# The causal mask of FoX attention: added in PSUM by VectorE in place of an identity product on TensorE

## Chip, core and metric

The kernel runs on one core of a Trainium2 chip. Times are device microseconds of one execution; a kernel's time is the median of its runs.

## What is computed

One block of a streaming encoder for 1024 tokens of width 1024: RMS norm, one input projection, attention heads and state-space (S5) heads side by side, one output projection, a mixture of 32 experts (the best four for each token), a gated per-layer embedding and a last norm. The change lies in the attention. Eight heads of 64 dimensions compute, for each block of 128 query rows,

```
logits = jnp.einsum('bqhd,bkhd->bhqk', q_i, k) * scale
logits = logits + c_i[..., :, None] - c_t[..., None, :]
logits = jnp.where(key_pos[None, :] <= q_pos[:, None], logits, -jnp.inf)
w = jax.nn.softmax(logits, axis=-1)
return jnp.einsum('bhqk,bkhd->bqhd', w.astype(v.dtype), v)
```

Here c is the cumulative sum of the log forget gates. Only the diagonal block of 128x128 (queries and keys of the same block) needs the mask within it; blocks beyond it aren't computed.

## The kernel before

The program is written by hand for each engine: five instruction streams, ordered by semaphores (`wait_ge`, `then_inc`). The attention stage handles 32 tiles. A tile is a pair of heads p and a query block i with i+1 key blocks; for each p the order of i is 0, 7, 1, 6, 2, 5, 3, 4 (`TILES`). Its scores come in units of up to 512 keys, one unit for i<4 and two for i≥4; a unit has two PSUM banks, one for each head of the pair, and two units' banks alternate.

A tile s passes through the engines like this:

- TensorE, `scores(s)`: q times k of both heads (L1717), and for the unit with the diagonal the mask (L1721). The unit's `s_mm` is raised by its last matmul. q carries a factor of −0.125, so the masked elements get +1e30 (`FAR`) and a minimum is the largest logit.
- VectorE, `row_low(s)` (L1198): for each unit and head one instruction reads the scores from PSUM, adds the gate sums (`cumb`), writes the result `sc` to SBUF and reduces its minimum into `low`. The profile calls it CUSTOM_DVE_ANT_0, with a small DVE_READ_ACCUMULATOR2_ANT behind it. It raises `low_ready`.
- ScalarE, `exp(s)` (L790): exp over the whole rows, one instruction for each head, with the sum `den`.
- VectorE, `recip(s)` (L1205): reciprocal of `den`; GpSimd (L626) multiplies the rows by it.
- TensorE, `turn_probs(s, part)` (L1735): 128x128 transposes into PSUM banks 4 and 5. ScalarE (L802) copies bank 4 to `probT`, VectorE's `turned_second` (L1216) copies bank 5. The next group of transposes into a bank waits for its copy.
- TensorE, `values(s)` (L1751): probT times v; VectorE's `heads_out` (L1224) copies the result to `attnT`.

The engines run ahead by three tiles. In turn s VectorE's queue holds recip(s+2), row_low(s+3), turned_second(s), heads_out(s−1), in this order; TensorE's holds scores(s+3), turn_probs(s, 0), values(s−1), turn_probs(s, 1); ScalarE's holds its copies of s and exp(s+3). GpSimd works on the GELU of the state-space heads in between. `link` raises `dve_chain` with an instruction and makes VectorE wait for it ahead of the next one.

The loop on VectorE:

```
recip(s + 2)
row_low(s + AHEAD)
turned_second(s)
heads_out(s - 1)
```

Of the kernel before, what the change touches and what calls it, by code (L numbers as in the profile page):

```python
# [23 lines left out]
ALU = mybir.AluOpType  # L24
ACT = mybir.ActivationFunctionType
F32 = mybir.dt.float32
BF16 = mybir.dt.bfloat16
# [5 lines left out]
P = 128  # L33
# [3 lines left out]
HEADS, DH = 8, 64  # L37
# [91 lines left out]
def build(nc, x_cm, x_tm, pT, small, consts, b_f, d_skipT, b_router, gains, w_in, w_glu, w_out,  # L129
          w_router, w_router_q, w_gu, w_dn, b_exp, b_gu, b_dn, w_ple_gate, w_ple_proj, out, hs, ys, cum):  # L130
    with ExitStack() as ctx:
        sem = {}

        def S(name):
            if name not in sem:
                sem[name] = ctx.enter_context(nc.semaphore(name))
            return sem[name]
# [12 lines left out]
        def at(name, shape, dt, offset):  # L150
            return nc.alloc_sbuf_tensor_at(name, shape, dt, offset=offset)

        def sb(name, shape, dt=F32):

            size = int(np.prod(shape[1:])) * (2 if dt == BF16 else 4)
            t = at(name, shape, dt, cursor[0])
            cursor[0] += (size + 31) // 32 * 32
            return t

        ps = ctx.enter_context(nc.psum_tensor("ps", [P, 8, 512], F32))  # L160
# [4 lines left out]
        ident = cst[:, O_ID:O_ID + P]  # L165
# [4 lines left out]
        tid = cst[:, O_TID:O_TID + 8]  # L170
        quad = cst[:, O_QD:O_QD + 1]
        ones = sb("ones", [P, P])
        ident_b = sb("ident_b", [P, P], BF16)
        mask_qk = sb("mask_qk", [P, P], BF16)
        bf = sb("bf", [8, 1])
        dsk = sb("dsk", [SC, NG])
# [43 lines left out]
        kA = at("kA", [P, HEADS // 2, T], F32, R_K)  # L220
# [130 lines left out]
        def scores_of(s):  # L351

            return sc01[:, s % 2] if s % 4 < 2 else sc23[:, s % 2]
# [620 lines left out]
        def _(dve):  # L974
            v = nc.vector
            chain = [0]

            def link(ins):

                chain[0] += 1  # L980
                ins.then_inc(S("dve_chain"), 1)
                dve.wait_ge(S("dve_chain"), chain[0])
# [150 lines left out]
            for n in range(2):  # L1133
                ins = v.tensor_scalar(rbc[:, 512 * n:512 * n + 512], ps[:, n, :], 1.0 / D, EPS, ALU.mult, ALU.add)
# [2 lines left out]
            v.reciprocal(rtok[:, :], rtok[:, :]).then_inc(S("rtok_ready"), 1)  # L1137
            dve.wait_ge(S("par_ld"), 16)
            dve.wait_ge(S("small_ld"), 80)
            v.tensor_copy(ident_b[:, :], ident)  # L1140
            dve.wait_ge(S("par_ld"), 16)
            dve.wait_ge(S("small_ld"), 80)
            link(v.tensor_copy(mask_qk[:, :], mask_f[:, :]))
            angles()
            coefficients()
# [3 lines left out]
            for i, un in enumerate(PROJ):  # L1149
# [20 lines left out]
                if un[0] in "kq":  # L1170
                    dst = kA if un[0] == "k" else qA
                    m, n = un[1:]
# [11 lines left out]
            def row_low(s):  # L1184


                p, i = TILES[s]
                if s >= 4:
                    dve.wait_ge(S("tr_mm"), 2 * UNITS[s - 3])
                for c in range(1 + (i >= 4)):  # L1190
                    un = UNITS[s] + c
                    w = min(512, (i + 1) * P - 512 * c)
                    dve.wait_ge(S("s_mm"), un + 1)
                    for a_ in range(2):
                        lo = low[:, s % 4, a_:a_ + 1]
                        if c:
                            dve.wait_ge(S("low_ready"), 2 * un - 1 + a_)
                        v.tensor_tensor_reduce(scores_of(s)[:, a_, 512 * c:512 * c + w], ps[:, 2 * (un % 2) + a_, 0:w],  # L1198
                                               cumb[:, p % 2, a_, 512 * c:512 * c + w], 1.0, lo if c else 3e38,
                                               ALU.add, ALU.min, lo).then_inc(S("low_ready"), 1)  # L1200
# [30 lines left out]
            for s in range(AHEAD):  # L1231
                row_low(s)
# [3 lines left out]
            for s in range(NT):  # L1236
                if s + 2 < NT:
                    recip(s + 2)
                if s and s + AHEAD < NT:
                    if (s + AHEAD) % 8 == 0:  # L1240
                        p = (s + AHEAD) // 8
# [24 lines left out]
            for n in range(8):  # L1266
                co, hf = n // 2, n % 2
# [126 lines left out]
            for c, w in enumerate(WIDTHS):  # L1394
                less = [i for i in range(NW) if WIDTHS[i] < w]
                if less:
                    i = max(less, key=lambda i: WIDTHS[i])
                    ins = v.tensor_tensor(cmask[:, c, 0:32], cown[:, i, 0:32], cown[:, c, 0:32], ALU.subtract)
                else:
                    ins = v.tensor_scalar(cmask[:, c, 0:32], cown[:, c, 0:32], -1.0, 1.0, ALU.mult, ALU.add)  # L1400
# [39 lines left out]
            for q in range(4):  # L1440
                c = slice(8 * q, 8 * q + 8)
# [150 lines left out]
        def _(pe):  # L1592
            m = nc.tensor
# [64 lines left out]
            for n in range(2):  # L1658
                ins = m.matmul(ps[:, n, :], ones[:, :], sqa[:, 512 * n:512 * n + 512], start=True, stop=True)
            ins.then_inc(S("sq_mm"), 1)  # L1660
            pe.wait_ge(S("h_ready"), KT)
            for t in range(4):
                for k in range(KT // 2, KT):
                    ins = u_step(t, k)
                ins.then_inc(S("pj_mm"), 1)
                if t == 1:
# [3 lines left out]
                    for c in range(16):  # L1670
                        toks = rbc[:, c:T:CH] if c < 8 else rbc[:, (c - 8) * P:(c - 7) * P]
                        ins = m.transpose(ps[:, (0, 1, 6, 7)[c // 4], (c % 4) * P:(c % 4) * P + P], toks, ident)
                    ins.then_inc(S("rtok_mm"), 1)
            for i, un in enumerate(PROJ):
# [5 lines left out]
                if un[0] == "u":  # L1680
                    for k in range(KT):
                        ins = m.matmul(ps[:, bank, :], hT[:, k, un[1]:T:CH], w_u[:, k, :], start=(k == 0), stop=(k == KT - 1))  # L1682
                elif un[0] == "v":
                    if un[1] == 0:
                        pe.wait_ge(S("wv_ld"), 32)
                    for k in range(KT):
                        ins = m.matmul(ps[:, bank, :], hT[:, k, un[1] * P:un[1] * P + P], w_v[:, k, :], start=(k == 0), stop=(k == KT - 1))  # L1687
                elif un[0] == "f":
                    for k in range(KT):

                        j = 32 * (k % 4)
                        ins = m.matmul(ps[j:j + 8, bank, :], wf[:, k, :], hT[:, k, 512 * un[1]:512 * un[1] + 512], start=(k < 4), stop=(k >= 4))
                else:
# [3 lines left out]
                    for k in range(KT):  # L1697
                        ins = m.matmul(ps[:, bank, :], w_[:, k, un[1] * P:un[1] * P + P], hT[:, k, 512 * un[2]:512 * un[2] + 512],  # L1698
                                       start=(k == 0), stop=(k == KT - 1))
# [5 lines left out]
            def scores(s):  # L1705


                p, i = TILES[s]
                for c in range(1 + (i >= 4)):
                    un = UNITS[s] + c  # L1710
                    if un >= 2:
                        pe.wait_ge(S("low_ready"), 2 * un - 2)
                    w = min(512, (i + 1) * P - 512 * c)
                    diag = (i * P) // 512 == c
                    for a_ in range(2):
                        hf = DH * a_
                        ins = m.matmul(ps[:, 2 * (un % 2) + a_, 0:w], qA[hf:hf + DH, p, i * P:i * P + P],  # L1717
                                       kA[hf:hf + DH, p, 512 * c:512 * c + w], start=True, stop=not diag)
                    if diag:
                        for a_ in range(2):  # L1720
                            ins = m.matmul(ps[:, 2 * (un % 2) + a_, w - P:w], ident_b[:, :], mask_qk[:, :], start=False, stop=True)  # L1721
                    ins.then_inc(S("s_mm"), 1)

            def turn_probs(s, part):
# [53 lines left out]
            for n in range(8):  # L1778
                co, hf = n // 2, n % 2
                if n >= 2:  # L1780
                    pe.wait_ge(S("gl_sig"), n - 1)
                for k in range(4):
                    ins = m.matmul(ps[:, 4 + n % 2, :], wglu[:, k, co * P:co * P + P], gT[:, k, hf * 512:hf * 512 + 512],  # L1783
                                   start=(k == 0), stop=(k == 3))
# [141 lines left out]
            for q in range(4):  # L1926
                pe.wait_ge(S("tok_ready"), 2 * q + 2)
                for c in range(8 * q, 8 * q + 8):
# [3 lines left out]
                    ins = m.matmul(ps[:, 1, at_:at_ + P], ohr[:, c, :], ohc[:, :, :].rearrange("p c n -> p (c n)")[:, lo:lo + P],  # L1932
                                   start=(c == 0), stop=(c == 31), skip_group_check=True)
# [4 lines left out]
            for r in range(4):  # L1938
                ins = m.matmul(ps[:, 6, nh * r:nh * r + nh], selq[:, r, :, :].rearrange("p a j -> p (a j)"), rowid[:, :], start=True, stop=True,
                               skip_group_check=True)  # L1940
# [75 lines left out]
            for i in range(16):  # L2016
# [4 lines left out]
                for k in range(2):  # L2021
                    ins = m.matmul(ps[:, 4 + i % 4, :], ppT[:, k, i // 2, :], wpp[:, k, 512 * (i % 2):512 * (i % 2) + 512], start=(k == 0), stop=(k == 1))
# [105 lines left out]
```

## Time and profile before

| | before |
|---|---|
| median of three runs | 2180.05 us (2179.83 to 2181.12) |
| profiled execution | 2180.62 us, of which span 2179.1 us |
| TensorE (PE) busy | 2120.1 us, 97% |
| VectorE (DVE) busy | 1005.8 us, 46% |
| ScalarE (ACT) busy | 374.4 us, 17% |
| GpSimd (POOL) busy | 599.2 us, 27% |
| mean granted TensorE clock | 0.993 |

The span goes from the first to the last instruction of the profiled execution. PE is TensorE's matmul side. The experts take the greater part of the span; the attention stage lies between about 275 and 406 us. In the rows a time in front is the start in us from the span's start; "[0.45 <-ACT sc L790]" behind a row says that the engine was idle for 0.45 us before it and what ended the wait. Durations of matmuls overlap with the next ones.

### The profile page before, as it was taken

The numbers are of one execution on the slowest core, as the hardware profiler recorded it, in microseconds if no ns is written. First come the engines' busy times: TensorE is split into PE (matmuls) and PEld (weight loads), VectorE is DVE, ScalarE is ACT, GpSimd is POOL, SyncE is SP. The second block draws the span as 40 slices with busy tenths as digits, with TensorE's granted clock in tenths as the row PEclk, the third lists the DMA queues.
The fourth block names the chain that finished last, engine by engine and source line by source line (L and its number), as shares of the span: only waits on it lengthen the run. The fifth ranks groups of instructions, "written<-read, shape, count | busy, mean of one in ns | idle before, by whom it ended". The sixth has DMA issues, their size and how long they took to land.

```text
span 2179.1 us, 53600 instructions
## 1 busy us (share of the span) xinstructions
PE 2120.1 (97%) x21898; PEld 1704.4 (78%) x21898; DVE 1005.8 (46%) x2155; ACT 374.4 (17%) x769; POOL 599.2 (27%) x905
## 2 busy tenths in 40 slices
PE   8999999999799999999999999999999999999998
PEld 5555566544478999999787889798999999999443
DVE  4665467534854544454343332623233333443474
ACT  3120056510411101000110100100000000000344
POOL 0465678300133122222212211213111231212420
PEclk9999999999999999999999999999999999999999
DMA  5100011512299999999999974989667888885740
GB/s 209 44 21 12 6 59 32 197 52 74 97 360 417 416 418 398 367 374 348 351 340 334 332 283 177 384 334 351 233 230 245 291 310 311 307 319 189 268 166 39
DMA packets 101816, 528.18 MB, mean 242 GB/s; under 512 B 22326, under 2 KB 26214, under 8 KB 49614
## 3 DMA queue, kind: packets, MB, share of 16 engines
q1 hardware_dynamic: 76894, 465.58, 56.9%
q0 software_dynamic: 24816, 61.12, 8.1%
q8 instruction: 75, 1.23, 0.2%
q14 instruction: 31, 0.25, 0.0%
HBM read 496.06 MB, written 27.30 MB: 240 GB/s over the span
## 4 chain that ended last, share of the span: by engine, by line
PE 90%; DVE 3%; issue 3%; ACT 2%; DMA 1%; POOL 1%; SPq 0%; POOLq 0%; DVEq 0%; ACTq 0%
PE ps L1963 23%; PE ps L1960 20%; PE ps L1978 14%; PE ps L1698 5%; PE ps L2001 4%; PE ps L2038 3%; PE ps L1991 3%; PE ps L1803 3%; PE ps L1687 3%; PE ps L1810 2%; PE ps L1717 1%; PE ps L1751 1%; PE ps L1783 1%; PE ps L1682 1%; PE ps L1735 1%
## 5 line engine op out<-in xcount | busy, mean ns | idle before, releaser
L1963 PE MATMUL ps<-xT,wg 128*64 128x112 f32 (+5 forms) x10752 | 504.5, 257 | 11.7 <-issue 8.3
L1963 PEld LDWEIGHTS ps<-xT,wg 128*64 128x64 f32 x10752 | 499.8, 138 | 20.3 <-issue 20.3
L1960 PE MATMUL ps<-xT,wg 128*128 128x144 f32 (+5 forms) x3072 | 434.8, 304 | 0.0
L1960 PEld LDWEIGHTS ps<-xT,wg 128*128 128x128 f32 x3072 | 430.0, 190 | 4.5 <-issue 1.3
L1510 DVE TENSOR_SCALAR gb<-ps,bcur 128x256 f32<-128x256 f32 x264 | 127.7, 484 | 559.9 <-PE ps L1963 287.5
L1978 PE MATMUL ps<-actT,wd 128*64 128x112 f32 (+6 forms) x3584 | 317.8, 278 | 0.0
L1978 PEld LDWEIGHTS ps<-actT,wd 128*64 128x64 f32 (+1 forms) x3584 | 313.8, 160 | 1.6
L920 ACT ACTIVATE sg<-gb 128x256 f32<-128x256 f32 x264 | 110.0, 417 | 1131.4 <-DVE gb L1510 1131.4
L639 POOL DMA_INDIRECT xg<-normalised_rows,rowc x184 | 178.5, 970 | 76.8 <-issue 49.1
L669 POOL COPY rowc<-rowq 128x8 uint32 (+1 forms) x34 | 6.4, 190 | 593.6 <-DVE xT L1475 591.0
L1500 DVE TENSOR_TENSOR tb<-gb,sg 128x256 f32<-128x256 f32 x264 | 112.2, 425 | 42.4 <-ACT sg L920 42.4
L1523 DVE STREAM_TRANSPOSE yb<-ps 128x1024 f32<-128x1024 f32 x20 | 25.0, 1250 | 230.4 <-PE ps L1978 230.4
L1511 DVE TENSOR_SCALAR ub<-ps,bcur 128x256 f32<-128x256 f32 x264 | 125.4, 475 | 0.0
L1503 DVE SCALAR_TENSOR_TENSOR actT<-ub,tb 128x256 f32<-128x256 f32 x264 | 112.1, 425 | 9.1
L2038 PE MATMUL ps<-wpg,xnT 128*128 128x512 f32 x256 | 112.4, 595 | 2.4 <-ACT xnT L933 2.4
L685 POOL DMA_DIRECT2D bin__188<-in_b_exp x33 | 18.9, 573 | 311.1 <-issue 311.1
L2001 PE MATMUL ps<-wd,actT 128*128 128x512 f32 x224 | 98.0, 595 | 0.0
L2038 PEld LDWEIGHTS ps<-wpg,xnT 128*128 128x128 f32 x256 | 47.5, 190 | 61.6 <-issue 54.5
L2001 PEld LDWEIGHTS ps<-wd,actT 128*128 128x128 f32 x224 | 42.0, 190 | 51.4 <-issue 51.4
L1475 DVE STREAM_TRANSPOSE xT<-xg 128x1024 f32<-128x1024 f32 x66 | 78.0, 1219 | 0.0
L696 POOL DMA_DIRECT2D expert_rows<-yb x80 | 46.6, 584 | 91.6 <-DVE yb L1525 69.9
L1991 PE MATMUL ps<-wd,actT 128*32 128x256 f32 x1024 | 57.7, 380 | 1.8 <-issue 1.8
(417 smaller groups left out, 2140.2 us busy)
## 6 DMA issues: line engine op xcount, KB each, us to landing
wg<-in_w_gu SPq DMA_DIRECT2D x264, 1024.0 KB, 7.3
wd<-in_w_dn SPq DMA_DIRECT2D x132, 1024.0 KB, 7.6
expert_rows<-yb POOLq DMA_DIRECT2D x60, 128.0 KB, 5.6
expert_rows<-yb POOLq DMA_DIRECT2D x28, 160.0 KB, 5.4
hT<-in_x_cm SPq DMA_DIRECT2D x8, 512.0 KB, 8.5
cumb<-gate_sums SPq DMA_DIRECT2D x4, 1024.0 KB, 4.8
x<-in_x_tm SPq DMA_DIRECT2D x1, 4096.0 KB, 13.7
wout<-in_w_out SPq DMA_DIRECT2D x1, 4096.0 KB, 21.0
```

The costliest lines, as they stand in the source:

```text
L639: g.indirect_dma_start(xg[:, half, DQ * r:DQ * r + DQ], None, hs[:, :], bass.IndirectOffsetOnAxis(ap=rows[:, r, half:half + 1], axis=0)).t ...
L920: a.activation(sg[:, f % 2, :], gb[:, f % 2, :], ACT.Sigmoid, scale=1.702).then_inc(S("sig_ready"), 1)
L1500: v.tensor_tensor(tb[:, f % 2, :], gb[:, f % 2, :], sg[:, f % 2, :], ALU.mult).then_inc(S("tb_ready"), 1)
L1503: v.scalar_tensor_tensor(actT[:, f, :], ub[:, f % 2, :], -6.0, tb[:, f % 2, :], ALU.max, ALU.mult).then_inc(S("act_ready"), 1)
L1510: v.tensor_scalar(gb[:, f % 2, :], ps[:, f % 2, 0:W], bcur[:, f:f + 1], 7.0, ALU.add, ALU.min).then_inc(S("g_ready"), 1)
L1511: v.tensor_scalar(ub[:, f % 2, :], ps[:, f % 2, W:2 * W], bcur[:, 8 + f:9 + f], 8.0, ALU.add, ALU.min).then_inc(S("gu_evac"), 1)
L1960: ins = m.matmul(ps[:, f % 2, g_ * W:g_ * W + w], wg[:, f, k, g_, :], xT[:, k, 0:w], start=(k == 0), stop=(k == KT - 1))
L1963: ins = m.matmul(ps[c:c + 64, f % 2, g_ * W:g_ * W + w], wg[:, f, k, g_, c:c + 64], xT[:, k, 0:w], start=(k == 0), stop=(k == KT - 1))
L1978: ins = m.matmul(ps[c:c + cols, 2 + o_ // 2, W * (o_ % 2):W * (o_ % 2) + w], wd[:, f, P * o_ + c:P * o_ + c + cols], actT[:, f, 0:w], star ...
L1991: ins = m.matmul(ps[GR * j:GR * j + GR, 2 + r // 2, 256 * (r % 2):256 * (r % 2) + 256], actT[:, f, GR * r:GR * r + GR], down_cols(f, j, 1) ...
L2001: ins = m.matmul(ps[:, 2 + c, :], actT[:, f, 0:P], down_cols(f, 2 * c, 2), start=(f == 0), stop=(f == FT - 1))
L2038: ins = m.matmul(ps[:, 2 + n, :], xnT[:, t % 2, k, :], wpg[:, k, n * 512:n * 512 + 512], start=(k == 0), stop=(k == KT - 1))
```

## The change

TensorE's two products of the identity with the mask go from `scores`; the scores' matmuls then end their group themselves. `row_low` gets one VectorE instruction ahead of the reductions of the unit with the diagonal: it adds the mask (bf16, the same for both heads) to the last 128 columns of both banks, in place in PSUM, and is linked, so the reduction waits for its end. The bf16 copy of the identity, `ident_b`, and its conversion are dropped.

```
@@ scalars, once @@
-            v.tensor_copy(ident_b[:, :], ident)
-            dve.wait_ge(S("par_ld"), 16)
-            dve.wait_ge(S("small_ld"), 80)
             link(v.tensor_copy(mask_qk[:, :], mask_f[:, :]))
@@ row_low @@
                     dve.wait_ge(S("s_mm"), un + 1)
+                    if (i * P) // 512 == c:
+                        at_diag = ps[:, 2 * (un % 2):2 * (un % 2) + 2, w - P:w]
+                        link(v.tensor_tensor(at_diag, at_diag, mask_qk[:, :].unsqueeze(1).to_broadcast([P, 2, P]), ALU.add))
                     for a_ in range(2):
@@ scores @@
-                    diag = (i * P) // 512 == c
                     for a_ in range(2):
                         hf = DH * a_
                         ins = m.matmul(ps[:, 2 * (un % 2) + a_, 0:w], qA[hf:hf + DH, p, i * P:i * P + P],
-                                       kA[hf:hf + DH, p, 512 * c:512 * c + w], start=True, stop=not diag)
-                    if diag:
-                        for a_ in range(2):
-                            ins = m.matmul(ps[:, 2 * (un % 2) + a_, w - P:w], ident_b[:, :], mask_qk[:, :], start=False, stop=True)
+                                       kA[hf:hf + DH, p, 512 * c:512 * c + w], start=True, stop=True)
                     ins.then_inc(S("s_mm"), 1)
```

VectorE's queue at the tiles i=5 and i=3, before: the first tile's four reductions (ISA is the reduction of L1198, the row behind it reads the accumulator), the copies of probT and attnT, the reciprocal, and the next tile's reductions and copy.

```order
L1198 ISA sc_96,low<-ps,cumb,low 128x256 [waits low_ready,s_mm]
L1198 ISA low 128x1
L1198 ISA sc_96,low<-ps,cumb,low 128x256 [waits low_ready]
L1198 ISA low 128x1
L1216 COPY probT<-ps 128x256 [waits tr_mm,pv_mm]
L1224 COPY attnT<-ps 128x16x8 [waits pv_mm]
L1205 RECIPROCAL rden<-den 128x2 [waits exp_done]
L1198 ISA sc_97,low<-ps,cumb 128x512 [waits s_mm,tr_mm]
L1198 ISA low 128x1
L1198 ISA sc_97,low<-ps,cumb 128x512
L1198 ISA low 128x1
L1216 COPY probT<-ps 128x384 [waits tr_mm,pv_mm]
```

The same place now, up to the second reduction of i=3 (lines behind the addition are one lower in the file, L1192 is the addition):

```order
L1192 TENSOR_TENSOR ps<-ps,mask_qk 128x2x128 [waits s_mm]
L1197 ISA sc_95,low<-ps,cumb,low 128x256 [waits low_ready,dve_chain]
L1197 ISA low 128x1
L1197 ISA sc_95,low<-ps,cumb,low 128x256 [waits low_ready]
L1197 ISA low 128x1
L1215 COPY probT<-ps 128x256 [waits tr_mm,pv_mm]
L1223 COPY attnT<-ps 128x16x8 [waits pv_mm]
L1204 RECIPROCAL rden<-den 128x2 [waits exp_done]
L1192 TENSOR_TENSOR ps<-ps,mask_qk 128x2x128 [waits s_mm,tr_mm]
L1197 ISA sc_96,low<-ps,cumb 128x512 [waits dve_chain]
L1197 ISA low 128x1
L1197 ISA sc_96,low<-ps,cumb 128x512
```

An addition has come in ahead of the second unit of i=5 and one between the reciprocal and the reductions of i=3; the waits for `s_mm` and `tr_mm` moved to it. The copy of 128x384 stands behind both.

TensorE's queue in the turn with the scores of i=3, before: scores, mask, transposes of the tile i=6, values of i=1, transposes again.

```order
L1717 MATMUL ps<-kA,qA 128x512 [waits low_ready]
L1717 MATMUL ps<-kA,qA 128x512
L1721 MATMUL ps<-mask_qk,ident_b 128x128 x2
L1735 MATMUL ps<-cst,sc_97 128x128 [waits ta_evac,pn_ready]
L1735 MATMUL ps<-cst,sc_97 128x128 x3
L1735 MATMUL ps<-cst,sc_97 128x128 [waits tb_evac,pn_ready]
L1735 MATMUL ps<-cst,sc_97 128x128 x2
L1751 MATMUL ps<-probT,vA 64x128 [waits at_evac,tb_evac,ta_evac]
L1751 MATMUL ps<-probT,vA 64x128 x3
L1735 MATMUL ps<-cst,sc_97 128x128 [waits ta_evac,pn_ready]
L1735 MATMUL ps<-cst,sc_97 128x128 x2
L1735 MATMUL ps<-cst,sc_97 128x128 [waits tb_evac,pn_ready]
```

The same turn now:

```order
L1715 MATMUL ps<-kA,qA 128x512 [waits low_ready]
L1715 MATMUL ps<-kA,qA 128x512
L1730 MATMUL ps<-cst,sc_96 128x128 [waits ta_evac,pn_ready]
L1730 MATMUL ps<-cst,sc_96 128x128 x3
L1730 MATMUL ps<-cst,sc_96 128x128 [waits tb_evac,pn_ready]
L1730 MATMUL ps<-cst,sc_96 128x128 x2
L1746 MATMUL ps<-probT,vA 64x128 [waits at_evac,tb_evac,ta_evac]
L1746 MATMUL ps<-probT,vA 64x128 x3
L1730 MATMUL ps<-cst,sc_96 128x128 [waits ta_evac,pn_ready]
L1730 MATMUL ps<-cst,sc_96 128x128 x2
L1730 MATMUL ps<-cst,sc_96 128x128 [waits tb_evac,pn_ready]
```

Only the row of the mask is gone. The last row is a transpose that waits for VectorE's copy of probT (`tb_evac`).

## Rows read from the trace of the kernel before

**Rows 1.** Windows: stage, one head pair, idle time and half-clock spell near its start.

```profile
core 0: us, PE busy (x) PEld busy (x) DVE busy (x) ACT busy (x) POOL busy (x), PEclk, DMA share, GB/s
275.00:406.00 131.00, 123.16 (x1170) 84.30 (x1169) 93.44 (x308) 79.17 (x187) 99.19 (x117) 0.99 0.19 54
324.46:354.69 30.23, 29.11 (x283) 19.88 (x281) 22.20 (x77) 20.18 (x48) 24.34 (x30) 1.00 0.11 36
286.40:288.80 2.40, 0.00 (x0) 0.00 (x0) 0.42 (x3) 2.30 (x6) 2.40 (x3) 1.00 0.05 20
289.80:293.20 3.40, 3.40 (x15) 2.37 (x16) 1.51 (x5) 1.87 (x5) 3.22 (x6) 0.51 0.00 0
```

**Rows 2.** Chain that ended last, 346 to 353 us: start, us, what.

```profile
346.64 0.69 DVE sc L1198
...
348.53 1.85 ACT sc L790 x3
...
350.84 0.23 DVE sc L1198
...
351.88 0.61 DVE probT L1216
352.50 0.14 issue
352.63 0.41 PE ps L1735 x2
```

**Rows 3.** Groups by form, 270 to 410 us: xcount, then busy us, mean ns.

```profile
L1721 PE MATMUL ps<-mask_qk,ident_b 128*128 128x128 bf16 x64 | 9.1, 224 | 0.0
...
L1198 DVE CUSTOM_DVE_ANT_0 sc<-ps,cumb 128x256 f32<-128x256 f32 x8 | 3.1, 422 | 2.9 <-PE ps L1721 2.9
```

**Rows 4.** Timeline of TensorE, 333 to 354 us: start, us, operation.

```profile
339.68 0.29 PE L1721 MATMUL ps<-mask_qk,ident_b 128*128 128x128 bf16 x2
339.80 1.05 PE L1735 MATMUL ps<-cst,sc 128*128 128x128 f32 x8
340.77 1.53 PE L1751 MATMUL ps<-probT,vA 128*64 128x128 f32 x24
```

**Rows 5.** Timeline of VectorE, 53 to 54.7 us; L1056 waits for L1055's end.

```profile
53.65 0.42 DVE L1054 TENSOR_TENSOR t<-cf,par 128x256 f32<-128x256 f32 x1
53.99 0.42 DVE L1055 TENSOR_TENSOR t<-cf,par 128x256 f32<-128x256 f32 x1
54.44 0.43 DVE L1056 TENSOR_TENSOR par<-t,t 128x256 f32<-128x256 f32 x1
```

**Rows 6.** Groups by form of VectorE, whole span.

```profile
L1511 DVE TENSOR_SCALAR ub<-ps,bcur 128x256 f32<-128x256 f32 x264 | 125.4, 475 | 0.0
...
L1500 DVE TENSOR_TENSOR tb<-gb,sg 128x256 f32<-128x256 f32 x264 | 112.2, 425 | 42.4 <-ACT sg L920 42.4
```

**Rows 7.** Timeline of VectorE behind tile i=5, 327.9 to 330 us.

```profile
327.98 0.17 DVE L1205 RECIPROCAL rden<-den 128x2 f32<-128x2 f32 x1 [0.45 <-ACT sc L790]
328.52 0.69 DVE L1198 CUSTOM_DVE_ANT_0 sc<-ps,cumb 128x512 f32<-128x512 f32 x1 [0.37 <-PE ps L1721]
...
329.74 0.55 DVE L1216 COPY probT<-ps 128x384 f32<-128x384 f32 x1
```

**Rows 8.** Timeline of TensorE: transposes behind that copy, two later groups of scores.

```profile
330.44 0.63 PE L1735 MATMUL ps<-cst,sc 128*128 128x128 f32 x4 [0.24 <-DVE probT L1216]
...
337.75 1.99 PE L1717 MATMUL ps<-kA,qA 64*128 64x512 f32 x8
...
345.36 1.77 PE L1717 MATMUL ps<-kA,qA 64*128 64x512 f32 x8
```

**Rows 9.** Timeline of VectorE behind tile i=4, 335.6 to 337 us.

```profile
335.67 0.17 DVE L1205 RECIPROCAL rden<-den 128x2 f32<-128x2 f32 x1 [0.32 <-ACT sc L790]
...
336.25 0.08 DVE L1198 DVE_READ_ACCUMULATOR2_ANT low<- 128x1 f32 x1
336.32 0.43 DVE L1216 COPY probT<-ps 128x256 f32<-128x256 f32 x1
```

**Rows 10.** Timeline of VectorE behind tile i=7, 343.4 to 344.5 us.

```profile
343.47 0.17 DVE L1205 RECIPROCAL rden<-den 128x2 f32<-128x2 f32 x1 [0.73 <-ACT sc L790]
...
344.28 0.28 DVE L1216 COPY probT<-ps 128x128 f32<-128x128 f32 x1
```

More of the change, by code:

```diff
@@ L172, in build @@
         ones = sb("ones", [P, P])
-        ident_b = sb("ident_b", [P, P], BF16)
         mask_qk = sb("mask_qk", [P, P], BF16)
```

## Prediction

> **What bounds the kernel now.** The change touches only the attention stage, so shares of the whole span say little and I began with the windows. The stage runs from 275 to 406 us: 131 us, TensorE busy for 123.16 (94%) and VectorE for 93.44 [rows 1]. It repeats. One head pair is eight tiles and takes 30.23 us (324.46 to 354.69), with TensorE busy for 29.11 us and VectorE for 22.20 [rows 1]. By these sums VectorE has 8 us to spare in each head pair and TensorE 1.1. A sum doesn't tell where idle time lies, so I went on to the chain of waits. Around the tiles i=6 and i=2 it leaves TensorE for 6 us: VectorE reduces, ScalarE exponentiates, VectorE takes the reciprocal, reduces tile i=2, copies probT, and only then does TensorE transpose [rows 2]. So the reader is to see a loop with one turn per tile: reduction, exp, reciprocal, the next tile's reduction. The copy that TensorE waits for stands in VectorE's queue behind that reduction.
>
> **What is removed.** 64 matmuls of the mask go, two in each of 32 tiles [rows 3]. Their 224 ns are mostly latency. What they take from TensorE is the distance from their start to the next group's: 339.68 to 339.80 [rows 4]. That is 0.12 us a tile, 32 × 0.12 = 3.8 us if nothing else changes. It counts only where TensorE is itself the limit; at a place where it waits for the copy of probT, an earlier arrival is only a longer wait. One conversion (ident_b, half of 128x256) at the start of the program goes as well; it can't be worth more than an operation of twice its size, 0.42 us [rows 5], and as the coefficients behind it wait for an exp of ScalarE I count it at nothing.
>
> **What is added.** 32 additions on VectorE over 128x256 elements, each with a wait of the next reduction for its end. No row shows VectorE writing PSUM, so I bound the price d per tile. Read from PSUM, the shape takes 422 ns as a reduction [rows 3]; the addition of two SBUF operands takes 425 [rows 6]. With a wait behind it the next operation starts 0.45 us later (53.99 to 54.44); without one, 0.34 (53.65 to 53.99) [rows 5]. Lower end of d: 0.34, if the wait cost nothing. Upper end: 475 ns for the slowest operation of this shape from PSUM [rows 6], plus the 0.03 between an end and a waiting start (54.41 to 54.44): 0.51. I take 0.45, because the addition is nearest to the TENSOR_TENSOR rows with a wait, and the reduction shows no surcharge for a PSUM source.
>
> The Trainium skill does put one on it ("VectorE: DVE Perf Modes", section on the TRN2 errata): 120 fixed cycles from PSUM against 58 from SBUF, at 0.96 GHz, thus an estimated 0.065 us more. This trace disagrees for reads (422 ns from PSUM, 425 from SBUF). By that rule d would be 0.52 and the sum 10.2 us, by the rows it is what follows.
>
> **Where d lands.** The addition stands ahead of the reduction whose end starts both exps. With i≥4 ScalarE starts as soon as the reduction has ended, so a whole d passes through the exps into the reciprocal; the next tile's addition comes behind that reciprocal, and then the copy of probT. The tiles thus work in pairs, and TensorE waits for the copy behind the second: 2d less the slack that the rows show. The copy's end reaches a transpose 0.14 us later (329.74 + 0.55 = 330.29 to 330.44; 351.88 + 0.61 to 352.63) [rows 7, 8, 2].
>
> - Pair (5,3), four times: the reciprocal runs at 327.98, and the reduction of i=3 could follow 0.15 later but starts at 328.52, when the mask matmul has ended [rows 7]. Slack 0.40; the transposes at 330.44 wait for the copy already [rows 8]. 2d − 0.40 = 0.50.
> - Pair (4,0), three times (the last tile, i=4, has no partner): the copy starts at 336.32, 0.07 after VectorE is free at 336.25, and ends at 336.75; with 0.14 it would allow transposes at 336.89 [rows 9]. The four that need it start about 337.26: the next group starts at 337.75 [rows 8], and four transposes take 0.49 (eight from 339.80 to 340.77 [rows 4]). Slack 0.36 + 0.07. 2d − 0.43 = 0.47.
> - Pair (7,1), three times: the copy ends at 344.56 [rows 10], allows 344.70, and the four start near 345.36 − 0.49 = 344.87 [rows 8]. 2d − 0.16 = 0.74. The reciprocal ahead of it waited 0.73 for the exps of i=7 [rows 10].
> - Pair (6,2), three times: no slack, both additions stand on the chain as it is [rows 2]. 2d = 0.90.
>
> The first pairs (7,1) and (6,2) don't count: from 286.40 to 288.80 TensorE is idle for 2.40 us while GpSimd, busy throughout, is late with its normalisation, and right after it TensorE runs at half clock (0.51 granted from 289.80 to 293.20, that is 1.2 GHz of 2.4) [rows 1]; VectorE's 0.9 us hides there. At every waiting place TensorE's own saving since the last wait disappears, so it is not subtracted. The sum is 4×0.50 + 3×0.47 + 3×0.74 + 3×0.90 = 8.3 us, in general 26d − 3.4; 0.1 for the last tile's copy makes 8.4. Nothing behind the stage hides it: by the code everything later hangs on the last tile's values. Against the profiled execution (span 2179.1, 2180.62 in all) that gives 2189.0; the median of the runs lies 0.57 below it, so I predict **2188.5 us**. The bounds of d give 5.5 and 10.0 us, 2185.6 and 2190.1.
>
> **Rivals.**
> - *VectorE's idle time takes it in.* 32 × 0.45 = 14.4 us fit in 131 − 93.4 = 37.6 us idle [rows 1], TensorE stays the limit and gains 3.8 us: 2176.2, not slower. It decides if the slack of every pair is 0.9 us or more. For it speaks TensorE's share of 94%; against it, that three pairs of a head pair show less than 0.5 and the fourth none. Chance 0.06, half of it for over 0.2% (should each mask matmul free the 0.22 us of its duration, 7 us). [...]
> - *Only the second addition counts.* If the first of a pair is taken in before the reciprocal, a place costs d less its slack. At (5,3), where the start then hangs on the scores, which come 0.12 earlier, it is 0.33, and 0.02, 0.29 and 0.45 at the others: 1.3 + 0.1 + 0.9 + 1.3 = 3.6 us, 2183.7, within 0.2%. Against it: the reciprocal waits for ScalarE in the pairs (0.45, 0.32 and 0.73 us [rows 7, 9, 10]). Chance 0.12.
> - *The addition is dearer*, with a penalty for writing PSUM and reading it at once: at d = 0.6 it is 12.2 us, 2192.3. Chance 0.06.
> - *The clock falls more often.* The half-clock spell of 3.4 us followed an idle time of 2.4 us; the new waits stay under 1 us. A spell costs at most 1.7 us; one more gives 2190.2, three 2193.6. Chance 0.07.
>
> **How the numbers follow.** My case has 0.69. A measurement of this kernel tells about 0.2% (4.4 us) from no change. Slower by over that: 0.69 + 0.06 + 0.07 = 0.82. Same: 0.12 + 0.03 = 0.15. Faster: 0.03. The range 2183.0 to 2193.0 takes in the second rival, the bounds of d, d = 0.6 and one or two more spells.
>
> **What would show it.** In the profile after: no L1721; 32 TENSOR_TENSOR on ps with 0.42 to 0.48 us, the reduction behind them 0.45 to 0.5 after their start; the eight tiles in about 32.8 us in place of 30.2 (30.2 + 0.50 + 0.47 + 0.74 + 0.90); about 8 us more idle time of TensorE before its transposes, released by VectorE's probT copy; the expert stage unchanged. A period of 30 us or less would refute the pairs; an unchanged period with a longer span would point at the clock.

## Result, and the profile after

The changed kernel takes **2189.77 us** (median of six runs, 2186.93 to 2191.90), the kernel before 2180.87 in the same comparison (six runs, 2179.83 to 2182.95). The ratio is 1.0041, 95% interval 1.0030 to 1.0051: 8.9 us slower, where 8.4 were forecast against the profiled execution. The sum came out right, but not all of its terms: in the profiled execution three half-clock spells came in, and 4.6 us came back in the experts, where I had expected nothing.

The page of the changed kernel, span and busy times:

```profile
span 2187.9 us, 53502 instructions
...
PE 2123.9 (97%) x21834; PEld 1706.5 (78%) x21834; DVE 1017.3 (46%) x2186; ACT 374.0 (17%) x769; POOL 599.4 (27%) x905
```

VectorE is busy for 11.5 us more. TensorE is too, for 3.8 us, with 64 products fewer: the first sign that its clock has to do with it. The totals don't show where the 8.8 us lie by which the span grew, so the windows come next: two periods of eight tiles, the place where TensorE waits longest in a period, and what its clock does behind it.

```profile
core 0: us, PE busy (x) PEld busy (x) DVE busy (x) ACT busy (x) POOL busy (x), PEclk, DMA share, GB/s
...
307.12:341.64 34.52, 30.91 (x276) 20.32 (x272) 24.97 (x85) 20.17 (x49) 26.79 (x32) 0.95 0.09 30
341.64:375.84 34.20, 30.23 (x264) 19.67 (x261) 25.01 (x86) 19.66 (x48) 26.26 (x32) 0.95 0.07 28
322.90:325.90 3.00, 1.08 (x10) 0.66 (x9) 2.16 (x7) 2.19 (x6) 2.26 (x3) 1.00 0.00 0
326.60:330.00 3.40, 3.40 (x14) 1.53 (x12) 2.53 (x9) 0.72 (x3) 3.22 (x5) 0.50 0.00 0
```

A period was 30.23 us at a clock of 1.00 [rows 1]. Now it is 34.20 to 34.52 at 0.95: more than the forecast 32.8. VectorE has 25.0 us of work in a period in place of 22.2, still 9 us short of it. The last row is new in kind: 3.40 us at a granted clock of 0.50, 1.2 of 2.4 GHz, and it comes in three of the four periods (326.63, 360.76 and 394.90 us).

Groups by form of the changed kernel, 270 to 420 us (the additions; the transposes):

```profile
L1730 PE MATMUL ps<-cst,sc 128*128 128x128 f32 x288 | 46.9, 293 | 16.3 <-POOL sc L625 6.0 <-ACT probT L801 5.3 <-DVE probT L1215 4.6
...
L1192 DVE TENSOR_TENSOR ps<-ps,mask_qk 128x256 f32<-128x256 f32 x32 | 13.7, 430 | 3.4 <-PE ps L1715 3.3
```

The addition takes 430 ns in place, within 5 ns of the same shape in SBUF [rows 6]. TensorE's idle time ahead of the transposes is 16.3 us; before, it was 6.6 in the same group, so 9.7 us were added.

VectorE's timeline of the changed kernel around the first such place, behind the tiles i=6 and i=2:

```profile
320.06 0.43 DVE L1192 TENSOR_TENSOR ps<-ps,mask_qk 128x256 f32<-128x256 f32 x1
320.52 0.62 DVE L1197 CUSTOM_DVE_ANT_0 sc<-ps,cumb,low 128x384 f32<-128x384 f32 x1
...
323.38 0.17 DVE L1204 RECIPROCAL rden<-den 128x2 f32<-128x2 f32 x1 [1.18 <-ACT sc L789]
323.46 0.43 DVE L1192 TENSOR_TENSOR ps<-ps,mask_qk 128x256 f32<-128x256 f32 x1
323.92 0.56 DVE L1197 CUSTOM_DVE_ANT_0 sc<-ps,cumb 128x384 f32<-128x384 f32 x1
...
324.88 0.69 DVE L1215 COPY probT<-ps 128x512 f32<-128x512 f32 x1
```

From the start of an addition to the reduction that waits for it are 0.46 us, both times. The first addition stands ahead of the exps (idle 1.18 until their end), the second between the reciprocal and the copy of probT. TensorE's timeline of the changed kernel there:

```profile
322.73 0.44 PE L1746 MATMUL ps<-probT,vA 128*64 128x128 f32 x4
324.49 0.63 PE L1730 MATMUL ps<-cst,sc 128*128 128x128 f32 x4 [1.32 <-ACT probT L801]
325.72 0.63 PE L1730 MATMUL ps<-cst,sc 128*128 128x128 f32 x4 [0.60 <-POOL sc L625]
```

and the same tiles in the kernel before, some 3 us earlier:

```profile
321.61 0.63 PE L1735 MATMUL ps<-cst,sc 128*128 128x128 f32 x4 [0.70 <-ACT probT L802]
322.41 0.63 PE L1735 MATMUL ps<-cst,sc 128*128 128x128 f32 x4 [0.18 <-DVE probT L1216]
```

The idle time grew from 0.88 to 1.92 us here: 0.62 behind ScalarE's copy, which stands behind the exps and so gets one addition (and what the mask's products no longer fill), and 0.42 behind VectorE's copy, which gets the second.

### The profile page after: what moved, and what is told of

The parts are those of the page before. It is cut to its first block, busy times and chain, and to the rows that moved or that the text cites. A ratio compares the mean times of both kernels' runs of the same rounds, so it can differ in the third digit from the quotient of the medians.

```text
span 2187.9 us, 53502 instructions
## 1 busy us (share of the span) xinstructions
PE 2123.9 (97%) x21834; PEld 1706.5 (78%) x21834; DVE 1017.3 (46%) x2186; ACT 374.0 (17%) x769; POOL 599.4 (27%) x905
## 4 chain that ended last, share of the span: by engine, by line
PE 88%; DVE 4%; issue 3%; ACT 2%; DMA 1%; POOL 1%; SPq 0%; POOLq 0%; DVEq 0%; ACTq 0%
PE ps L1958 23%; PE ps L1955 20%; PE ps L1973 14%; PE ps L1697 5%; PE ps L1996 4%; PE ps L2033 3%; PE ps L1986 3%; PE ps L1798 3%; PE ps L1686 3%; PE ps L1805 2%; PE ps L1715 1%; PE ps L1778 1%; PE ps L1681 1%; DVE x L1537 1%; PE ps L1730 1%
## 5 line engine op out<-in xcount | busy, mean ns | idle before, releaser
L1958 PEld LDWEIGHTS ps<-xT,wg 128*64 128x64 f32 x10752 | 497.2, 138 | 18.7 <-issue 18.7
L1958 PE MATMUL ps<-xT,wg 128*64 128x112 f32 (+5 forms) x10752 | 501.5, 256 | 10.4 <-issue 7.0
L1510 DVE TENSOR_SCALAR ub<-ps,bcur 128x256 f32<-128x256 f32 x264 | 125.5, 475 | 0.0
L1730 PE MATMUL ps<-cst,sc 128*128 128x128 f32 x288 | 46.9, 293 | 16.3 <-POOL sc L625 6.0
```

Of the source, the lines that this page charges most:

```text
L1510: v.tensor_scalar(ub[:, f % 2, :], ps[:, f % 2, W:2 * W], bcur[:, 8 + f:9 + f], 8.0, ALU.add, ALU.min).then_inc(S("gu_evac"), 1)
L1958: ins = m.matmul(ps[c:c + 64, f % 2, g_ * W:g_ * W + w], wg[:, f, k, g_, c:c + 64], xT[:, k, 0:w], start=(k == 0), stop=(k == KT - 1))
```

## The experiments

Two theories stood at first. The **pairs** (the prediction's): two additions on the loop through VectorE and ScalarE, less the slack of each place, and nothing else. The **clock**: the new waits make TensorE run at half clock, and this is a good part of the loss. The experts gave a third question. "End of the stage" is the end of the last tile's values, 405.97 us in the profile of before; all differences are to that profile, tile by tile, so that the stage's start, the periods and the spells can be told apart.

**Both kernels again.**

> The kernel before, profiled once more, unchanged. My reading of the first pair of traces: the attention stage ends 13.6 us later after the change (8.6 us of waits and 5.0 us for three more half-clock spells), and the experts' two memory-bound passes give back 4.6 us by chance. Chance theory: the attention stage lasts 130.7 us again (values end within 0.5 us of 405.97) while the sum of the two memory-bound expert passes (30.1 and 33.0 us in the first trace of before) moves by a us or more. Rival, the giving back is a mechanism that follows from the later start: both passes last as in the first trace, within 0.3 us.

2181.76 us (one run). Its stage ends 1.33 later: the half-clock spell at 288 us lasts 6.83 us in place of 3.41. All of the difference is there by the second tile and stays the same for the other 30. So a tile's time reproduces to 0.02 us but for the start, where the longer spell costs 1.3. The chance theory of the experts had asked for an end within 0.5 us and for passes that differ by 1 us or more; they differ by 0.54 (63.15 and 62.61 us, table below). It failed on both.

> The changed kernel, profiled once more, unchanged, timed in five rounds. Both theories: about 2189.8 us. Attention theory: last values near 419.5, period of eight tiles 34.2 to 34.5 us, three spells of half clock behind the waits at the pair (6,2). Chance theory for the experts: their two memory-bound passes differ from 27.5 and 31.0 us by a us or more in sum; rival (mechanism): they don't.

2189.43 us, ratio 1.0042 (1.0029 to 1.0056). The stage ends 12.35 later than before's, against 13.57 in the first profile of the same kernel. This one has two spells in its periods (358.70, 392.83), the first had three; up to 322 us the two differ by 0.26. The experts' two passes differ by 0.92 us from the first profile's, where the chance theory wanted 1 or more.

**Fill the wait.** Twelve transposes of the identity into a free bank, in the turns of i=7 from the second pair of heads on:

```diff
                     values(s - 1)
+                if s > 8 and TILES[s][1] == 7:
+                    pe.wait_ge(S("at_evac"), s - 1)
+                    for _ in range(12):
+                        m.transpose(ps[:, 6 + s % 2, 0:P], ident, ident)
```

> The changed kernel with 12 extra transposes of the identity on TensorE, at the three places where it waits about 1.4 us for the copy of tile i=7 (ahead of its second group of transposes); they write a PSUM bank that the next values overwrite, and leave all waits as they are. Clock theory: TensorE's idle time there is what makes the clock fall; the three spells at 326.6, 360.8 and 394.9 vanish and the time falls by up to 5 us, to about 2185. Rival (the spells come from elsewhere or cost nothing): spells stay, time 2189.8 or up to 4 us more, for the added work.

Timeline of TensorE in this kernel, the second of the three places:

```profile
357.19 1.53 PE L1768 MATMUL ps<-cst 128*128 128x128 f32 x12
358.58 0.63 PE L1730 MATMUL ps<-cst,sc 128*128 128x128 f32 x4
359.80 0.63 PE L1730 MATMUL ps<-cst,sc 128*128 128x128 f32 x4 [0.59 <-POOL sc L625]
```

The wait of 1.32 us is filled, that of 0.6 is left as it was, and no period has a spell (the ones at 361 and 395 were expected to go; the run's first, at 288 us, is the long one). The three periods and the last tiles, from 322 us on, cost 7.60 us (10.67 − 3.07); in the two profiles of the changed kernel they cost 11.31 and 10.35. So the waits alone are worth 7.6 us there, three spells 3.7 and two 2.75: 1.2 to 1.4 each. At the spell itself 1.59 is lost (2.55 in place of 0.96 from one tile to the next), and 0.35 comes back at the following wait. So the clock is a second cause, and the spells are gone where this idle time is filled. That is one profiled execution with three places, against two with five spells in six. The kernel gained nothing in all, where up to 5 us were expected (2190.36 us, ratio 1.0038, 1.0025 to 1.0052); its experts say why, below.

**The second addition moved away from the copy.** The additions of i<4 go to the front of the turn, ahead of the reciprocal, and the reduction waits for them later:

```diff
             for s in range(NT):
+                if s and s + AHEAD < NT and TILES[s + AHEAD][1] < 4:
+                    mask_early(s + AHEAD)
                 if s + 2 < NT:
```

> The changed kernel with the addition of the tiles i<4 issued ahead of the reciprocal instead of behind it; all 32 additions stay on VectorE. Pair theory: the second addition of a pair leaves the chain where VectorE waits for ScalarE anyway, wholly at (6,2), 0.3 us at (7,1), little at (5,3) and (4,0): 3 x 0.45 + 3 x 0.3 = 2.3 us less waiting, and if the shorter wait at (6,2) lets the clock stand, up to 5 us more: 2187.5 without, 2182.5 with. Rival (VectorE's busy time is what costs, wherever the additions stand): no change, 2189.8.

2183.00 us over 11 runs, ratio 1.0009 (1.0000 to 1.0018). Timeline of VectorE at the same place; the addition runs in time in which VectorE waited for the exps:

```profile
319.62 0.49 DVE L1186 TENSOR_TENSOR ps<-ps,mask_qk 128x256 f32<-128x256 f32 x1
320.97 0.17 DVE L1215 RECIPROCAL rden<-den 128x2 f32<-128x2 f32 x1 [0.86 <-ACT sc L789]
```

and TensorE:

```profile
322.08 0.63 PE L1743 MATMUL ps<-cst,sc 128*128 128x128 f32 x4 [1.32 <-ACT probT L801]
322.91 0.63 PE L1743 MATMUL ps<-cst,sc 128*128 128x128 f32 x4 [0.20 <-DVE probT L1226]
```

From 322 us on the stage costs 3.98 us. That is my second rival, "only the second addition counts", turned round and built into a kernel: one addition at each place. Of its 3.6 us, 3.0 belong to this part. The first wait is still 1.32, the second is back from 0.60 to 0.20, and there is no spell anywhere in the stage. Behind an idle time of 1.52 no spell came in three places; behind 1.92 one came in five of six, and in seven of nine with the last experiment's (`pad`). Idle time alone doesn't decide: at the stage's start this run waits 2.95 us, as the changed kernel does ahead of its spell at 289 us, and has none.

**One half of the tiles only.** `only_high` adds on VectorE for i≥4 and leaves the mask on TensorE for i<4; `only_low` the other way round:

```diff
-                    if (i * P) // 512 == c:
+                    if (i * P) // 512 == c and i >= 4:
@@ scores @@
+                    if (i * P) // 512 == c and i < 4:
+                        for a_ in range(2):
+                            ins = m.matmul(ps[:, 2 * (un % 2) + a_, w - P:w], ident_b[:, :], mask_qk[:, :], start=False, stop=True)
```

> The addition on VectorE only for the tiles i>=4 (first of each pair); TensorE keeps the mask product for i<4. Pair theory: only one d of 0.46 us per pair, which the slack swallows at (5,3) and (4,0) and mostly not at (7,1) and (6,2): per period of eight tiles about 0.05 + 0.02 + 0.30 + 0.46 = 0.8 us over the 30.2 of before, where all additions gave 2.7 without a spell; attention stage 3 to 4 us longer than before, time 2183 to 2184. Rival (each addition costs the same 0.3 us wherever it stands): half of the change's waits, stage 4.8 us longer.

> The addition on VectorE only for the tiles i<4 (second of each pair), behind the reciprocal; TensorE keeps the mask product for i>=4. Pair theory: 0.35 + 0.05 + 0.30 + 0.46 = 1.2 us per period over 30.2, stage 4 to 5 us longer, time about 2184.5; together with the other half less than the 9.6 us of the whole, since the slack counts twice when the halves are apart. Rival (same cost for each): stage 4.8 us longer and the halves add up to the whole.

2184.77 (ratio 1.0014, 1.0005 to 1.0024) and 2184.57 us (1.0011, 1.0002 to 1.0021). From 322 us on they cost 3.01 and 2.78 us: 5.8 together, where both additions in one kernel without spells cost 7.6. By the prediction's slacks one addition at each place costs 3 × 0.05 + 2 × 0.02 + 2 × 0.29 + 3 × 0.45 = 2.1 us in this part, and two cost 6.6. The slack is used up once, by whichever comes first; so the halves don't add up, as the pairs say and a fixed price for each addition doesn't.

**Moved and halved.** `low_early` is `early` for i<4 with TensorE's mask for i≥4; `early012` the same for i=0, 1, 2 alone.

> The addition on VectorE for the tiles i<4 alone and ahead of the reciprocal; TensorE keeps the mask product for i>=4. Pair theory: it runs while VectorE waits for ScalarE; what is left is 0.35 us at (5,3), and TensorE saves 16 x 0.12 us less what disappears in waits: period 30.2 to 30.4 us, time 2180 to 2182, no more than before within the measurement. Rival (VectorE's busy time or a contention in PSUM costs): about 2184, as with the same additions behind the reciprocal.

> The addition on VectorE for i = 0, 1 and 2 alone, ahead of the reciprocal, without the tiles i=3 whose scores come too late for it; TensorE keeps the mask product for i>=3. Pair theory: no addition is left on a chain that TensorE waits for, TensorE has 12 products less to do of which some are hidden: stage 0 to 1.4 us shorter than before, time 2179.5 to 2181, a tie or 0.05% faster. Rival (additions cost wherever they stand): 12 x 0.3 us, 2184.

2181.10 us (0.9996, 0.9986 to 1.0005) and 2181.53 (1.0000, 0.9991 to 1.0009). The stage ends 2.79 later in the one, some 2 of it at its start (a spell of 6.83 us in place of 3.41), and 0.16 earlier in the other. Even with additions that run while VectorE waits anyway, the best versions only equal the kernel before.

**The mask left out.** The additions of the changed kernel are skipped, so queries see the later keys of their own block:

```diff
-                    if (i * P) // 512 == c:
+                    if False:
```

> No mask at all: neither TensorE's product nor VectorE's addition (the causal mask within the diagonal blocks is left out). It shows what the removal alone is worth. Pair theory: at (5,3) and (6,2) TensorE waits for the chain through VectorE, which starts 0.12 us sooner with the scores; all 32 x 0.12 us count unless ScalarE or the copies bind: 2 to 3.8 us, 2177 to 2179. Rival (TensorE isn't the limit in this stage): under 1 us, 2180.

Other values send the tokens to other experts, which lengthens the expert stage by some 117 us (2298.08 us in all), so only the attention stage can be compared. It ends 0.70 us earlier than before's. But its spell at the start lasts 6.83 us, as in `before_again`, and against that profile it ends 2.03 us earlier. So TensorE lost 3.8 us of work there and won 0.7 or, with like spells, 2.0: about half. Its idle time ahead of the transposes is 7.1 us, in place of 6.6.

The run also corrects a reading. Timeline of all engines in it, same place, a row each of GpSimd, VectorE and TensorE:

```profile
321.26 2.01 POOL L625 TENSOR_SCALAR sc<-sc,rden 128x896 f32<-128x896 f32 x2 [0.42 <-DVE rden L1204]
...
322.07 0.69 DVE L1215 COPY probT<-ps 128x512 f32<-128x512 f32 x1
...
322.91 0.63 PE L1730 MATMUL ps<-cst,sc 128*128 128x128 f32 x4 [0.17 <-DVE probT L1215]
```

The transposes start at 322.91 while GpSimd works until 323.27, so they don't need it. In the changed kernel the same wait of 0.60 is put down to GpSimd, because its end (325.65) is the last before the start (325.72); VectorE's copy ended at 324.88 + 0.69 = 325.57, and 0.14 behind it is 325.71. It is the copy that is waited for, with the 0.14 that the prediction used.

**Both masks.** VectorE's addition as in the change, and TensorE's products as before (the mask is added twice, which leaves the result as it is):

> Both masks: TensorE's product as before and VectorE's addition as after the change. It shows the addition without the removal. Pair theory: where TensorE waits for VectorE the products are hidden, elsewhere they count; 1 to 3 us above the changed kernel in the attention stage, time 2190 to 2193. Rival (the removal saved nothing even in part): same as the changed kernel, 2189.5.

2195.55 us, ratio 1.0067 (1.0052 to 1.0082). The stage ends 12.84 later, with two spells (359.36, 393.50), within 0.5 of the changed kernel again. TensorE's 64 products hardly count in the stage beside the additions; 1 to 3 us and a time of 2190 to 2193 were expected. But the kernel is 6 us slower than the changed one: 4.1 to 5.0 of it in the experts' two passes, where it lacks the give-back.

**A delay alone.** The kernel before, and behind the last values 105 transposes of the identity:

```diff
             values(NT - 1)
+            pe.wait_ge(S("low_ready"), 2 * UNITS[NT])
+            for _ in range(105):
+                m.transpose(ps[:, 0, 0:P], ident, ident)
```

> The kernel before, with 105 transposes of the identity on TensorE between the last values and the gating products: about 12 us of busy TensorE, nothing else changed, so everything behind the attention stage starts 12 us later with no other cause. Chance theory: the experts' memory-bound passes last 30 and 33 us on average as before, and the time is 2181 + 12 = 2193. Rival (a later start of the experts is given back by a mechanism): the passes last 27.5 to 28 and 31 to 31.7 us and the time is 2188 to 2190.

They take 11.45 us (407.28 to 418.73) and the kernel 11.0 us more (2192.22, ratio 1.0045, 1.0031 to 1.0059). A stage that ends later is not made up for by what comes behind it. The give-back must be something else in the changed program.

**Where the give-back lies.** I compared the experts pass by pass (a pass goes from the start of one run of gate and up products to the start of the next and has the down products behind it; here the runs of L1963 before and L1958 after). 27 of the first 30 have the same length in both to 0.01 us, and so they have in every kernel with the reference's mask. Between 1362 and 1393 us the pass takes 30.14 before and 27.52 after, between 1482 and 1516 us 33.01 and 31.03: 4.6 us. The first of the two as the chain that ended last shows it, kernel before:

```profile
1362.96 5.16 PE ps L1963 x170
1368.12 0.29 issue
1368.41 3.89 PE ps L1963 x126
1372.31 2.92 issue
1375.23 5.46 PE ps L1963 x127
1380.69 0.69 issue
```

and the changed kernel:

```profile
1376.41 10.70 PE ps L1958 x361
1387.11 2.09 issue
1389.20 3.95 PE ps L1958 x127
1393.14 2.30 issue
```

TensorE stands still and nothing in the profile ends the wait ("issue"). The waits come every 127 matmuls, each with its weight load. Before, one of 2.92 us is followed by 127 matmuls in 5.46 us in place of 3.95. A window of the kernel before on this stretch shows the half clock behind it, with the DMA engines full:

```profile
1375.20:1378.60 3.40, 3.37 (x65) 3.37 (x65) 1.60 (x4) 0.42 (x1) 0.00 (x0) 0.50 1.03 431
```

The DMA view of the kernel before over the pass, 1362.9 to 1393.1 us, has a queue of the program itself:

```profile
q1 hardware_dynamic: 1389, 10.18, 86.0%
...
q8 instruction: 5, 0.08, 1.0%
```

Five packets of 16 KB. The Trainium skill tells of them ("Runtime: NRT & Kernel Launch", Instruction fetch mechanics): each engine's program is refilled in 16 KiB blocks of 256 instructions by a queue of its own, at a cost that is "mostly hidden". The distance agrees (127 matmuls and 127 weight loads). That it is hidden doesn't, where the weights fill the queues: 0.3 to 2.9 us a block. The packets' times bear this out. In the two passes of `before`, `after` and `pad` (the last experiment) each of the 18 waits of 0.29 us or more ends 2.2 to 2.6 us after a packet of this queue has started; for the wait of 2.92 us, the packet starts at 1372.90 and TensorE goes on at 1375.23.

If these are the waits, 64 products taken out of the program, or others put in, must move the waits. In each trace I counted the matmuls from the start of the pass to its first waits of over 0.3 us, and set beside it the length of the two passes:

| kernel | products fewer ahead of the experts | first pass, waits behind | second pass, waits behind | both passes, us |
|---|---|---|---|---|
| before | 0 | 297, 424, 550 | 279, 406, 532 | 63.15 |
| before again | 0 | 297, 424, 550 | 279, 406, 532 | 62.61 |
| both | 0 | 170, 297, 424, 550 | 279, 406, 532 | 63.56 |
| after | 64 | 361, 488 | 342, 469 | 58.55 |
| after again | 64 | 361, 488 | 342, 469 | 59.47 |
| early | 64 | 234, 361, 488 | 342, 469 | 60.72 |
| only_high | 32 | 202, 329, 456 | 184, 311, 438 | 62.37 |
| only_low | 32 | 202, 329, 456, 581 | 184, 311, 438 | 61.47 |
| low_early | 32 | 202, 329, 456, 581 | 184, 311, 438 | 62.00 |
| early012 | 24 | 194, 321, 448, 574 | 176, 303, 430 | 62.38 |
| fill | 64 − 36 = 28 | 198, 325, 452, 577 | 180, 307, 434 | 62.47 |
| delay | −105 | 193, 320, 447, 573 | 175, 302 | 63.42 |

The places follow from the count to within a matmul or two: 279 + 32 = 311, 279 + 24 = 303, 297 + 64 = 361, 297 − 105 + 127 = 319. The length follows less closely: with 64 products fewer the passes take 58.55, 59.47 and 60.72 us in three profiles, with the old count 62.61 to 63.56 in four (`pad` among them), and in between 61.47 to 62.47. The last experiment sets the count back without touching the stage: the changed kernel with 32 small fp32 products at its start (L1595; the trace counts each as two).

```diff
             pe.wait_ge(S("ones_ready"), 1)
+            for _ in range(32):
+                m.matmul(ps[:, 0, 0:16], ones[:, :], ones[:, 0:16], start=True, stop=True)
```

> The changed kernel with 32 small fp32 products of a tile of ones on TensorE at the very start, while it waits for its first input; they appear as 64 weight loads and 64 matmuls, as many as the mask took, so all code behind the attention stage lies where it lay before the change. Code theory: the experts' two passes in which TensorE waits for pieces of its own program (27.5 to 27.8 and 31.0 to 31.7 us in all three traces with the changed program, without the half-clock spell) go back to the lengths of the program before, 33.0 us for the later one and 28 or more for the earlier; the attention stage stays 11 to 13.6 us longer than before; time 2191.5 to 2194. Rival (those passes vary by chance, or with the start of the stage): later pass anywhere from 31 to 33 us and time 2189.5.

The chain of this kernel in the first pass:

```profile
1389.26 3.95 PE ps L1960 x127
1393.21 1.77 issue
1394.98 3.94 PE ps L1960 x127
1398.92 2.32 issue
```

The waits are back behind 171, 298, 425 and 550, and 279, 406 and 532 matmuls, and the passes take 30.31 and 32.77 us: before's length, 63.08 in all. In this profiled execution the give-back is gone: the distance to before is 19.66 us ahead of the two passes and 19.59 behind them. One part went otherwise than expected. The products were not hidden in the wait for the first input, the stage starts 6.4 us later, and so the time (2198.09 us, ratio 1.0071, 1.0058 to 1.0085) can't be compared directly. Less 6.4 it is 2191.7, which is 9.8 us above the kernel before of the same comparison (2181.94), where the changed kernel has 8.9. So the times don't show the lost 4 us; with runs from 2194.75 to 2200.96, the profiled one the slowest, they can't exclude them either. What moves with the count, the waits and with them the passes, is shown by the traces alone.

## Why the prediction held, step by step

- **What bounds the stage:** right. The loop from reduction over exp to reciprocal and copy does, not TensorE's 94%. Taking 3.8 us off TensorE gained 0.7, or 2.0 against the profile with a like spell (`none`).
- **d = 0.45:** measured 0.46, the operation 430 ns. No surcharge for PSUM. The upper bound was read from the wrong row: the slowest operation of this shape from PSUM is L1510 with 484 ns, not L1511 with 475; it moves the bound by 0.01.
- **The pairs**, from the profile of `fill`, where no spell falls between the tiles: (5,3) 0.53 to 0.56 four times (0.50 forecast), (7,1) 0.88 (0.74), (6,2) 0.96 to 0.98 (0.90), (4,0) 0.59, 0.95 and 0.59 (0.47), the last tile 0.38 (0.1). These are 10.3 us. Of them 0.9 are no loss: in twelve turns between the waits TensorE gains 0.07 to 0.08, its own saving, and the next wait takes it back, as the prediction has it ("disappears"). `both`, which keeps the products, has neither, and shows the bare price of the pairs where no spell falls: (5,3) 0.43 to 0.49, (4,0) 0.50 to 0.52 three times, (7,1) 0.81, (6,2) 0.89. So three slacks were read rightly to 0.05 or so, that of (7,1) 0.07 too large. With 0.2 at the start the stage without spells is 9.6 us, as `after_again` less its two spells (12.35 − 2.75) has it, against 8.4. The terms that were mis-sized are one place of (4,0) and the rest of that pair (together 0.5), the last tile (0.3), (7,1) (0.2) and the start (0.2). Why (4,0) loses 0.95 in one period of the changed kernel, and 0.51 there in `both`, I can't say.
- **The start hides its pairs (7,1) and (6,2):** right, +0.19 behind them in `after_again`.
- **"The new waits stay under 1 us", hence the clock at 0.07:** this step failed. Each single growth is under 1 us. But at (6,2) they come on top of waits that were there, on both sides of four transposes: 1.92 us idle out of 2.6. Three spells cost 3.7 us, two 2.75. The bound on their price, 1.7, held.
- **"Nothing behind the stage hides it", "the expert stage unchanged":** failed, by a mechanism that isn't in the stage. The program is 64 products shorter, and the waits for its blocks fall at other places of two passes. Against the first profile of before these are 4.6, 3.7 and 2.4 us shorter in the three profiles with the shorter program (`after`, `after_again`, `early`).
- **The sum.** In the profiled execution: 9.9 of waits, 3.7 of spells, 4.6 back, make 9.0 of the 8.8 us by which the spans differ; the remainder lies between 406 and 642 us, where half-clock spells fall differently (+1.4 ahead of the first expert, −1.5 in it). 8.4 was met because the two things that I left out are of about the same size and opposite sign. That is luck. `both`, the same additions without the shorter program, has no such offset and loses 14.4 us.
- **What the trace should show:** one L1192 per tile, the price and the 9.7 us of idle time were there; the period was 34.2 to 34.5 instead of 32.8, most of the difference a spell (`fill`, without one, has 32.9 and 33.3). Some of the idle time stood under other names than VectorE's copy: under ScalarE's, a second path for the first addition that I had not named, and under GpSimd's, wrongly.

The rivals: VectorE's idle time takes nothing in (the period grew); only the second addition counts in `early`, not here; the addition isn't dearer; the clock came in addition to my case, not in its place. Open are why a spell comes in two periods of one execution and three of another, why the start has none in `early` and `only_low` after the same idle time, and what makes a block late by 0.3 us in one place and by 2.9 in another.

## What to carry to other kernels

Work taken from the busiest engine is worth what it waits less, not what it works less: look for the loop through the other engines, take its slack place by place, and charge an operation put into it once for each time that the loop passes it. Add new waits to those that stand next to them before you call the clock safe. In a difference of under 1%, compare the stages that the change doesn't touch as well: here they gave back 4.6 of the 13.6 us that the stage had lost, for no reason that the diff shows. A kernel with the same additions and the old length of program (`both`) showed what they cost where nothing is given back.

## What was not expected of the hardware

- Where the DMA engines are full (share 0.95 to 1.03), TensorE stands still for 0.3 to 2.9 us every 127 matmuls with weight loads. In this kernel 24 to 105 products more or less in the attention stage or ahead of it moved these waits by as many matmuls 1 ms later; the two passes concerned took between 58.55 and 63.56 us.
- Behind 1.92 us of idle time, on both sides of four transposes, 3.4 us at half clock came in seven of nine places (`after`, `after_again`, `pad`), behind 1.77 in two of three (`both`), behind 1.52 in none of three (`early`). At the stage's start 2.4 to 3.0 us of idle time were followed by half clock in twelve of fourteen profiles. Such a spell cost 1.2 to 1.4 us in a stage whose TensorE waits anyway, and 1.5 in the one place of the experts read above (127 matmuls in 5.46 us in place of 3.95).
- Adding in place in PSUM took 430 ns for 128x256, nearly the same as in SBUF (425); the additions moved forward in `early` took 454.
